# The routing ahead of an expert-choice layer: a table of bits on GpSimd, ties summed ahead of counts, the first expert's slot comparisons on two engines, and index products tile by tile

## The chip, the cores and the metric

The kernel runs on one core of a Trainium2 chip. The metric is device time in microseconds, as the median of several runs; lower is better. Matrix products run on TensorE (PE), elementwise work on VectorE (DVE), ScalarE (ACT) and GpSimd (POOL); SyncE (SP) issues most of the transfers.

## The reference, cut to what matters

The program is one layer of a diffusion backbone for 2048 latent and 128 context tokens of width 1024, all in fp32: modulation, a mixer of a long convolution and a retention branch, then an expert-choice mixture of 16 experts, then a final RMS norm. The change touches only the routing of the mixture:

```python
def ec_moe(h, p):
    T = B * L
    xt = h.reshape(T, D)
    aff = jax.nn.softmax((xt @ p["w_router"]).astype(F32), axis=-1)
    cap = (EC_CAPACITY_FACTOR * T) // N_EXPERTS          # 256 latent, 16 context tokens
    vals, idx = lax.top_k(aff.T, cap)                    # each expert picks its tokens
    xs = xt[idx]
    hid = silu(einsum("ecd,edf->ecf", xs, w_e_gate)) * einsum("ecd,edf->ecf", xs, w_e_up)
    ye = einsum("ecf,efd->ecd", hid, w_e_down) * vals[..., None]
    return zeros((T, D)).at[idx.reshape(-1)].add(ye.reshape(-1, D))
```

So for each expert the kernel must find the 256 latent and 16 context tokens of the largest probability, lowest token first among equals, and their numbers as a list that a gathering transfer can use.

## The kernel before

The program is a row of phases, each a block in which every engine has its own instruction stream; the streams meet only in semaphores. A helper class `Steps` counts one semaphore per list of named steps: `give` raises it once at the start by two rounds' worth, `inc` marks a step done, `at` is the value to wait for. All of the change lies in the last phase, `phase_experts`, and there ahead of the loop over experts.

The order there is fixed by hand, by the order of the instructions on each engine and the waits between them:

1. Entry. Each engine raises its own semaphores with `give`. DVE copies the probabilities into `arr` (three tiles of 128x128: latent, latent, context) and makes `spread` (step `as`); PE transposes the four tiles (L2697, L2698), so that a partition now holds an expert and an eighth of its tokens; DVE copies them to `prob`, sums `few`, and sets `thr`, `cand` and `bit`.
2. Threshold search, 15 rounds of two bits (`DIGITS`). The threshold is built as the bit pattern of a float. In a round DVE counts, for three candidate thresholds, how many latent probabilities reach each (L2940, three times, with the count accumulated into `cnt`), while POOL compares the context ones with theirs (L3162, three times 128x16, into `reach`). PE adds over partitions with a matrix `seg`: sixteen matmuls for the context (L2702) and one for the latent counts (L2705), in this order. DVE has meanwhile shifted `bit` right by two (L2943) and formed `rest`, the threshold so far with the bits of the three next candidates (L2946); when PE's sums are there it compares them with the capacities (L2949 for the context, L2952 for the latent ones), which gives the digit, then `step` (L2955), the next `cand` (L2957) and `thr` (L2959). POOL and DVE both wait for `cand`.
3. Above and ties. DVE counts what lies above the threshold (`gl`, `gc`, L2965), PE adds the counts (`above`, L2709), DVE subtracts them from the capacities (L2968), marks the ties (`tl`, `tc`, L2970) and makes running sums of them (L2976); the ends of these (L2980) go through PE (`ahead`), and L2985 takes that off `need` too (step `lim`). Then come the choice of ties, the running sums of all chosen tokens, their offsets, and a transpose on PE into `pos`: for each token and expert, how many chosen ones come up to it.
4. The first expert. For each of 16 tiles of 128 latent tokens DVE compares the 256 slot numbers with the position of the tile's tokens (`passed`, L3008, 128x256), then once 128x16 for the context (L3012). PE multiplies each result by ones, which counts for every slot the tokens below it and so gives the token's number (`index`, 32 matmuls L2722 and one L2724, all behind the last comparison). DVE copies the numbers to integers (`numbers`, L3023, L3024). POOL then does a one-element addition (`carry`, L3170), which serves as a step of its own stream, and starts three gathering transfers (L3183). The gathered tokens are transposed, split into high and low parts, and the products of expert 0 begin.
5. While the gather runs DVE makes the comparisons for the second expert. For later experts they are spread over the loop two experts ahead, three at a time.

Of the kernel before, what the change touches and what calls it, by code (L numbers as in the profile page):

```python
# [6 lines left out]
I32 = mybir.dt.int32  # L7
BF16 = mybir.dt.bfloat16
F32R = mybir.dt.float32r
ALU = mybir.AluOpType  # L10
# [4 lines left out]
P = 128  # L15
# [13 lines left out]
EPS = 1e-6  # L29
# [2489 lines left out]
def phase_experts(nc, d, s):  # L2519


    DIGITS = 15
    with ExitStack() as ctx:
# [10 lines left out]
        bit = sb("bit", [P, 2, 3], I32)  # L2534
# [59 lines left out]
        RB = counted("dve_bits", ["count", "bit", "next", "mc", "ml", "step", "cand", "thr"])  # L2594
        PB = counted("pool_bits", ["reach"])
        R1 = counted("dve_slots", ["gl", "gc", "need", "tl", "tc", "s0", "s1", "e0", "e1", "lim", "k0", "k1",
                                          "sel", "p0", "p1", "f0", "f1", "off", "q0", "q1", "pos", "ones"])
        QB, QC = counted("pe_bits", ["sum"]), counted("pe_bits_context", ["sum"])
        Q1 = counted("pe_route", ["prob", "above", "ahead", "slots", "pos"])
# [59 lines left out]
        with nc.Block() as block:  # L2659
# [29 lines left out]
            def _(pe):  # L2689
# [17 lines left out]
                for name, ready, half, src in (("above", "gc", 0, cnt[:, 0:2]), ("ahead", "e1", 1, ends[:]), ("slots", "f1", 1, ends[:])):  # L2707
                    pe.wait_ge(R1.sem, R1.at(0, ready))
                    pe.matmul(pi[:, 0:2], seg_b[:, P * half:P * half + P], src, start=True, stop=True)\  # L2709
                      .then_inc(*Q1.inc(name))  # L2710
# [6 lines left out]
                def index(e):  # L2717
                    pe.wait_ge(VM.sem, VM.at(e, "mc"))
                    pe.wait_ge(VI.sem, VI.at(e - 1, "i2"))
                    for half in range(2):  # L2720
                        for n in range(NLAT):
                            pe.matmul(pi[:, half:half + 1], below[:, n, P * half:P * half + P], ones[:],  # L2722
                                      start=(n == 0), stop=(n == NLAT - 1))
                    pe.matmul(pi[0:CCAP, 2:3], below_c[:], ones[:], start=True, stop=True).then_inc(*PI.inc("ids"))  # L2724
# [182 lines left out]
            def _(v):  # L2907
                for steps in (VG, VM, VI, VX, VK, VD, VW, VF, V0):
                    steps.give(v)
                v.sem_inc(VX.sem, KT)  # L2910
                v.memset(rms[:], 1.0).then_inc(*VF.inc("one"))
                v.memset(eps[:], EPS).then_inc(*VF.inc("eps"))
                for steps in (R0, RB, R1):
                    steps.give(v)
# [3 lines left out]
                for b in range(2):  # L2918
# [4 lines left out]
                                band[:].unsqueeze(1).broadcast_to([P, NE, 8]), ALU.mult).then_inc(*R0.inc("as"))  # L2923
                v.wait_ge(Q1.sem, Q1.at(0, "prob"))
# [4 lines left out]
                for j in range(3):  # L2929
                    v.memset(cand[:, :, j:j + 1], (j + 1) << (2 * DIGITS - 2))  # L2930
# [355 lines left out]
```

## Time and profile before

| what | value |
|---|---|
| median of 3 runs | 3420.57 us (3418.08 to 3425.08) |
| the profiled execution's own time | 3417.76 us |
| its span | 3415.5 us |
| PE busy | 3189.0 us (93%) |
| DVE busy | 1602.9 us (47%) |
| ACT busy | 1269.8 us (37%) |
| POOL busy | 375.8 us (11%) |

The span is the time from the first to the last instruction of one profiled execution; "busy" is the time in which an engine had an instruction in work. Instructions that only raise or await a semaphore are not busy time. The expert phase begins at about 2037 us of the span and the products of the first expert at about 2105 us; they take most of what follows. Times in the rows below are microseconds from the span's start; "mean" and the three numbers with slashes are nanoseconds.

### The profile page before, as it was taken

The numbers are of one execution on the slowest core, as the hardware profiler recorded it, in microseconds if no ns is written. First come the engines' busy times: TensorE is split into PE (matmuls) and PEld (weight loads), VectorE is DVE, ScalarE is ACT, GpSimd is POOL, SyncE is SP. The second block draws the span as 40 slices with busy tenths as digits, with TensorE's granted clock in tenths as the row PEclk, the third lists the DMA queues.
The fourth block names the chain that finished last, engine by engine and source line by source line (L and its number), as shares of the span: only waits on it lengthen the run. The fifth ranks groups of instructions, "written<-read, shape, count | busy, mean of one in ns | idle before, by whom it ended". The sixth has DMA issues, their size and how long they took to land. (4 is left out here: it accounts for less than half of the span.)

```text
span 3415.5 us, 51856 instructions
## 1 busy us (share of the span) xinstructions
PE 3189.0 (93%) x19543; PEld 2717.1 (80%) x19543; DVE 1602.9 (47%) x2955; ACT 1269.8 (37%) x1953; POOL 375.8 (11%) x358
## 2 busy tenths in 40 slices
PE   7899998999889699999989975999999999999996
PEld 2488887899745689989987764898888888899995
DVE  5423322433246442333225557555555555565556
ACT  4743442422243031222114542444444443444435
POOL 1011111000034100000000002111111111111122
PEclk9899999999999799999999986999999999999998
DMA  8633333322199761432115443555555555555557
GB/s 332 243 120 111 105 107 100 134 67 71 58 363 353 247 193 58 129 99 88 69 51 201 158 163 130 185 191 184 187 179 183 175 175 175 180 198 195 192 207 274
DMA packets 282678, 565.68 MB, mean 166 GB/s; under 512 B 23464, under 2 KB 162472, under 8 KB 278329
## 3 DMA queue, kind: packets, MB, share of 16 engines
q1 hardware_dynamic: 258063, 503.84, 42.7%
q0 software_dynamic: 15456, 54.88, 5.4%
q10 hardware_dynamic: 8976, 4.46, 0.4%
q8 instruction: 123, 2.02, 0.2%
q14 instruction: 60, 0.49, 0.0%
HBM read 434.45 MB, written 128.64 MB: 165 GB/s over the span
## 5 line engine op out<-in xcount | busy, mean ns | idle before, releaser
L71 PE MATMUL experts_bank<-experts_xT_high,experts_w_high_gu 128*128 128x272 f32 x2048 | 598.0, 292 | 6.2 <-DVE experts_w_low_gu L3032 5.5
L73 PE MATMUL experts_bank<-experts_xT_high,experts_w_low_gu 128*128 128x272 f32 x2048 | 591.9, 289 | 0.0
L72 PE MATMUL experts_bank<-experts_xT_low,experts_w_high_gu 128*128 128x272 f32 x2048 | 589.6, 288 | 0.0
L71 PEld LDWEIGHTS experts_bank<-experts_xT_high,experts_w_high_gu 128*128 128x128 f32 x2048 | 385.9, 188 | 19.5 <-issue 12.3
L72 PEld LDWEIGHTS experts_bank<-experts_xT_low,experts_w_high_gu 128*128 128x128 f32 x2048 | 387.1, 189 | 3.9
L73 PEld LDWEIGHTS experts_bank<-experts_xT_high,experts_w_low_gu 128*128 128x128 f32 x2048 | 386.0, 188 | 0.0
L3032 DVE TENSOR_TENSOR experts_w_low_gu<-experts_w_raw_gu,experts_w_high_gu 128x1024 fp32r<-128x1024 f32 x256 | 302.6, 1218 | 12.5 <-ACT experts_w_high_gu L2828 12.5
L2828 ACT ACTIVATE experts_w_high_gu<-experts_w_raw_gu 128x1024 fp32r<-128x1024 f32 x256 | 257.1, 1047 | 14.5 <-DMA experts_w_raw_gu<-in_w_stream 14.5
L71 PE MATMUL merge_pg<-merge_hT_high,merge_w_gates_high 128*128 128x436 f32 (+1 forms) x640 | 232.1, 363 | 12.0 <-DVE merge_hT_low L2097 12.0
L72 PE MATMUL merge_pg<-merge_hT_low,merge_w_gates_high 128*128 128x436 f32 (+1 forms) x640 | 231.3, 361 | 0.0
L73 PE MATMUL merge_pg<-merge_hT_high,merge_w_gates_low 128*128 128x436 f32 (+1 forms) x640 | 230.9, 361 | 0.0
L71 PE MATMUL experts_bank<-experts_w_high_d,experts_hid_high 128*128 128x512 f32 x512 | 209.7, 410 | 6.3 <-DVE experts_hid_low L3107 6.3
L72 PE MATMUL experts_bank<-experts_w_low_d,experts_hid_high 128*128 128x512 f32 x512 | 203.7, 398 | 0.0
L73 PE MATMUL experts_bank<-experts_w_high_d,experts_hid_low 128*128 128x512 f32 x512 | 202.2, 395 | 0.0
L71 PE MATMUL hyin_pz<-hyin_hT_high,hyin_w_high 128*128 128x436 f32 (+1 forms) x480 | 176.6, 368 | 16.1 <-DVE hyin_hT_low L1358 16.1
L3101 DVE TENSOR_TENSOR experts_full<-experts_bank,experts_act_g 128x256 f32<-128x256 f32 x128 | 54.4, 425 | 286.1 <-issue 143.9
L2071 ACT ACTIVATE merge_gate<-merge_pg 128x436 f32<-128x436 f32 (+1 forms) x80 | 41.4, 532 | 363.8 <-PE merge_pg L73 363.7
L73 PE MATMUL hyin_pz<-hyin_hT_high,hyin_w_low 128*128 128x436 f32 (+1 forms) x480 | 173.3, 361 | 0.0
L72 PE MATMUL hyin_pz<-hyin_hT_low,hyin_w_high 128*128 128x436 f32 (+1 forms) x480 | 173.1, 361 | 0.0
L3170 POOL TENSOR_TENSOR experts_spare<-experts_spare 128x1 f32<-128x1 f32 x46 | 51.3, 1127 | 1034.6 <-DVE experts_ye L3133 874.2
L2882 ACT ACTIVATE experts_hid_high<-experts_full 128x256 fp32r<-128x256 f32 x128 | 53.6, 419 | 283.5 <-DVE experts_full L3101 281.8
L2873 ACT ACTIVATE experts_act_g<-experts_bank 128x272 f32<-128x272 f32 x128 | 50.9, 398 | 289.1 <-PE experts_bank L73 286.8
(395 smaller groups left out, 6586.5 us busy)
## 6 DMA issues: line engine op xcount, KB each, us to landing
experts_w_raw_gu<-in_w_stream SPq DMA_DIRECT2D x256, 512.0 KB
experts_w_raw_d<-in_w_stream SPq DMA_DIRECT2D x128, 512.0 KB, 6.7
filters_wm<-in_w_mod SPq DMA_DIRECT2D x12, 2048.0 KB, 11.9
merge_hT<-scratch_hT SPq DMA_DIRECT2D x32, 436.0 KB, 7.3
scratch_h<-out_row SPq DMA_DIRECT2D x17, 520.0 KB, 3.0
x_early<-in_xs SPq DMA_DIRECT2D x17, 512.0 KB, 5.4
scratch_hT<-tokens_hT SPq DMA_DIRECT2D x17, 512.0 KB, 4.2
scratch_qkT<-tokens_qkT SPq DMA_DIRECT2D x17, 512.0 KB, 2.8
```

Source lines behind the costliest of these rows:

```text
L71: pe.matmul(out, lhs[0], rhs[0], start=start, stop=False)
L72: pe.matmul(out, lhs[0], rhs[1], start=False, stop=False)
L73: return pe.matmul(out, lhs[1], rhs[0], start=False, stop=stop)
L2071: act.activation(gate[:, c % 2, j, 0:n], pg[:, c % 2, j, 0:n], ACT.Sigmoid)\
L2828: act.activation(wh[kind][:, n % RINGS[kind], :], raw[kind][:, r, :], ACT.Copy).then_inc(*AW.inc(name))
L2873: act.activation(act_g[:], pg[:, 0:SLOTS], ACT.Silu).then_inc(*AG.inc(f"g{f}"))
L2882: act.activation(hh[:, f % 2, :], full[:, f % 2, :], ACT.Copy).then_inc(*AH.inc(f"h{f}"))
L3032: v.tensor_tensor(wl[kind][:, w, :], raw[kind][:, n % STAGES[kind], :], wh[kind][:, w, :].bitcast(F32), ALU.subtract).then_inc(*VW.inc(name))
L3101: v.tensor_tensor(full[:, f % 2, :], pu[:, 0:CAP], act_g[:, 0:CAP], ALU.mult).then_inc(*VG.inc(f"m{f}"))
L3170: g.tensor_tensor(spare[:, column:column + 1], spare[:, 0:1], spare[:, 0:1], ALU.add)\
```

## The change

There are five edits, all ahead of the loop over experts.

- The three bits of every round come from a table `unit` (14 rounds by 3 values) that POOL fills with 42 memsets at the start of the phase. The tile `bit`, its three memsets and its shift in every round are gone; DVE waits for the table once, ahead of the first round. The last round uses the last row again, as its `rest` is not read for another threshold.
- DVE raises only the semaphore `R0` before it begins; its other increments come behind the step `as`, two more behind `ones`, and the memsets of `rms` and `eps` behind the first expert's index copy. POOL's increments `CG` and `CP` come ahead of its rounds.
- The ties are marked and summed ahead of the counts. PE's sum of the ties goes to `pi`, that of the counts to another place in PSUM, `pn`.
- The first expert's comparisons are split: tiles 0 to 11 on DVE, 12 to 15 (`SPLIT` = 4) on POOL; the context's stays on DVE. PE waits for each tile by itself in its first sixteen matmuls.
- POOL's `carry` ahead of the first gather is replaced by an increment at the start.

```diff
+    SPLIT = 4
-        bit = sb("bit", [P, 2, 3], I32)
+        unit = sb("unit", [P, DIGITS - 1, 3], I32)
...
+        units, pool_below, dve_below = sem("units"), sem("pool_below_first"), sem("dve_below_first")
...
@@ PE
-                for name, ready, half, src in (("above", "gc", 0, cnt[:, 0:2]), ("ahead", "e1", 1, ends[:]), ("slots", "f1", 1, ends[:])):
+                for name, ready, half, src, to in (("ahead", "e1", 1, ends[:], pi), ("above", "gc", 0, cnt[:, 0:2], pn), ("slots", "f1", 1, ends[:], pi)):
                     pe.wait_ge(R1.sem, R1.at(0, ready))
-                    pe.matmul(pi[:, 0:2], seg_b[:, P * half:P * half + P], src, start=True, stop=True)\
+                    pe.matmul(to[:, 0:2], seg_b[:, P * half:P * half + P], src, start=True, stop=True)\
                       .then_inc(*Q1.inc(name))
...
                 def index(e):
-                    pe.wait_ge(VM.sem, VM.at(e, "mc"))
+                    if e:
+                        pe.wait_ge(VM.sem, VM.at(e, "mc"))
                     pe.wait_ge(VI.sem, VI.at(e - 1, "i2"))
                     for half in range(2):
                         for n in range(NLAT):
+                            if e == 0 and half == 0:
+                                if n < NLAT - SPLIT:
+                                    pe.wait_ge(dve_below, n + 1)
+                                else:
+                                    pe.wait_ge(pool_below, n - NLAT + SPLIT + 1)
                             pe.matmul(pi[:, half:half + 1], below[:, n, P * half:P * half + P], ones[:],
                                       start=(n == 0), stop=(n == NLAT - 1))
+                    if e == 0:
+                        pe.wait_ge(dve_below, NLAT - SPLIT + 1)
...
@@ DVE
-                for steps in (VG, VM, VI, VX, VK, VD, VW, VF, V0):
-                    steps.give(v)
-                v.sem_inc(VX.sem, KT)
-                v.memset(rms[:], 1.0).then_inc(*VF.inc("one"))
-                v.memset(eps[:], EPS).then_inc(*VF.inc("eps"))
-                for steps in (R0, RB, R1):
-                    steps.give(v)
+                R0.give(v)
                 v.memset(arr[:], 0.0).then_inc(*R0.inc("zero"))
...
+                for steps in (RB, R1, VG, VM, VI, VX, VK, VD, VW, VF, V0):
+                    steps.give(v)
                 v.wait_ge(Q1.sem, Q1.at(0, "prob"))
...
-                    mm = v.memset(bit[:, :, j:j + 1], (j + 1) << (2 * DIGITS - 2))
+                v.wait_ge(units, 1)
...
-                    v.tensor_single_scalar(bit[:], bit[:], 2, ALU.logical_shift_right).then_inc(*RB.inc("bit"))
                     v.wait_ge(RB.sem, RB.at(i - 1, "thr"))
-                    v.wait_ge(RB.sem, RB.at(i, "bit"))
-                    v.tensor_tensor(rest[:], thr[:].unsqueeze(2).broadcast_to([P, 2, 3]), bit[:], ALU.bitwise_or)\
+                    v.tensor_tensor(rest[:], thr[:].unsqueeze(2).broadcast_to([P, 2, 3]),
+                                    unit[:, min(i, DIGITS - 2), :].unsqueeze(1).broadcast_to([P, 2, 3]), ALU.bitwise_or)\
...
-                for n, name in enumerate(("gl", "gc")):
-                    v.tensor_scalar(parts(over, n), parts(prob, n), t(n), 0.0, ALU.is_gt, ALU.add,
-                                    accum_out=cnt[:, n:n + 1]).then_inc(*R1.inc(name))
-                v.wait_ge(Q1.sem, Q1.at(0, "above"))
-                v.tensor_tensor(need[:], caps[:], pi[:, 0:2], ALU.subtract).then_inc(*R1.inc("need"))
...
                 running(tie, "s", "e")
+                for n, name in enumerate(("gl", "gc")):
+                    v.tensor_scalar(parts(over, n), parts(prob, n), t(n), 0.0, ALU.is_gt, ALU.add,
+                                    accum_out=cnt[:, n:n + 1]).then_inc(*R1.inc(name))
                 v.wait_ge(Q1.sem, Q1.at(0, "ahead"))
-                v.tensor_tensor(need[:], need[:], pi[:, 0:2], ALU.subtract).then_inc(*R1.inc("lim"))
+                v.tensor_tensor(need[:], caps[:], pi[:, 0:2], ALU.subtract).then_inc(*R1.inc("need"))
+                done("need")
+                v.wait_ge(Q1.sem, Q1.at(0, "above"))
+                v.tensor_tensor(need[:], need[:], pn[:, 0:2], ALU.subtract).then_inc(*R1.inc("lim"))
...
                 done("ones")
+                v.sem_inc(VX.sem, KT)
+                v.sem_inc(VM.sem, NLAT + 1)
...
+                def passed_first():
+                    for n in range(NLAT - SPLIT):
+                        v.tensor_scalar(below[:, n, :], slot[:], pos[:, n % 2, n // 2:n // 2 + 1], None, ALU.is_ge)\
+                         .then_inc(dve_below, 1)
+                    v.tensor_scalar(below_c[:], slot[:, 0:CCAP], pos[:, 2, 0:1], None, ALU.is_ge).then_inc(dve_below, 1)
...
-                for n in range(NLAT):
-                    passed(0, n)
-                passed_context(0)
+                passed_first()
                 numbers(0, 0, 0)
+                v.memset(rms[:], 1.0).then_inc(*VF.inc("one"))
+                v.memset(eps[:], EPS).then_inc(*VF.inc("eps"))
...
@@ POOL
                 PB.give(g)
+                for i in range(DIGITS - 1):
+                    for j in range(3):
+                        mm = g.memset(unit[:, i, j:j + 1], (j + 1) << (2 * (DIGITS - 2 - i)))
+                mm.then_inc(units, 1)
+                CG.give(g)
+                CP.give(g)
+                g.sem_inc(*CG.inc("carry"))
...
-                    carry(CG, "carry", 1)
+                    if e:
+                        carry(CG, "carry", 1)
...
+                g.wait_ge(R1.sem, R1.at(0, "pos"))
+                for n in range(NLAT - SPLIT, NLAT):
+                    g.tensor_scalar(below[:, n, :], slot[:], pos[:, n % 2, n // 2:n // 2 + 1], None, ALU.is_ge)\
+                     .then_inc(pool_below, 1)
                 g.wait_ge(stored, 1)
                 gather(0, 0)
```

## Rows read from the trace of the kernel before

**Rows 1.** Busy time of the engines in three stretches; columns in the first line.

```profile
core 0: us, PE busy (x) PEld busy (x) DVE busy (x) ACT busy (x) POOL busy (x), PEclk, DMA share, GB/s
2038.40:2092.40 54.00, 12.88 (x298) 10.52 (x298) 45.99 (x285) 2.11 (x2) 13.54 (x45) 0.50 0.24 81
2092.40:2105.00 12.60, 6.00 (x58) 5.13 (x58) 9.70 (x25) 3.59 (x5) 3.19 (x4) 0.50 0.67 212
2105.00:2108.90 3.90, 3.90 (x18) 3.90 (x19) 3.02 (x9) 2.06 (x3) 2.74 (x3) 0.52 0.32 78
```

**Rows 2.** Timeline of DVE, entry: start, us, engine, line, operation [idle before].

```profile
2038.88 0.38 DVE L2915 MEMSET experts_ye<- 128x384 f32 x1 [0.33 <-issue]
...
2039.72 0.28 DVE L2922 TENSOR_TENSOR experts_ye<-aff,band 128x128 f32<-128x128 f32 x1
2041.22 0.56 DVE L2925 COPY experts_ye<-experts_bank 128x384 f32<-128x384 f32 x1 [1.21 <-PE experts_bank L2698]
...
2042.09 0.48 DVE L2940 TENSOR_SCALAR_CACHE_REDUCE experts_ye<-experts_ye,experts_cand 128x256 f32<-128x256 f32 x1
```

**Rows 3.** Line 44, `give`, at the entry: count, ns min/median/max, first and last start.

```profile
L44 DVEq EVENT_SEMAPHORE  x12: 21/21/21, 2037.5 to 2038.7; - x12
L44 PEldq EVENT_SEMAPHORE  x8: 51/51/51, 2037.5 to 2038.7; - x8
```

**Rows 4.** Timeline of POOL, its first instruction in the phase.

```profile
2037.45 0.10 POOL L3152 MEMSET experts_spare<- 128x4 f32 x1 [882.36 <-POOLq L2224]
```

**Rows 5.** Busy time by stretch: four memsets of POOL at the program's start.

```profile
0.26:0.45 0.19, 0.00 (x0) 0.00 (x0) 0.00 (x0) 0.00 (x0) 0.19 (x4) 1.00 0.00 0
```

**Rows 6.** Timeline of one round, DVE, POOL and PE (one of fifteen).

```profile
2044.25 0.17 DVE L2957 TENSOR_TENSOR experts_cand<-experts_step,experts_rest 128x6 int32<-128x6 int32 x1
2044.33 0.15 DVE L2959 TENSOR_TENSOR experts_thr<-experts_thr,experts_step 128x2 int32<-128x2 int32 x1
...
2044.51 0.90 POOL L3162 TENSOR_SCALAR experts_reach<-experts_few,experts_cand 128x16 bf16<-128x16 f32 x3 [1.43 <-DVE experts_thr L2959]
...
2045.47 0.59 PE L2702 MATMUL experts_bank<-experts_reach,seg 128*128 128x3 bf16 x16 [1.72 <-POOL experts_reach L3162]
...
2045.66 0.17 DVE L2943 TENSOR_SCALAR experts_bit<-experts_bit 128x6 int32<-128x6 int32 x1
2045.93 0.17 DVE L2946 TENSOR_TENSOR experts_rest<-experts_thr,experts_bit 128x6 int32<-128x6 int32 x1
2046.10 0.16 DVE L2949 TENSOR_SCALAR_CACHE_REDUCE experts_met<-experts_bank 128x3 f32<-128x3 f32 x1
```

**Rows 7.** Timeline of DVE: first count, tie tests, `lim`.

```profile
2077.70 0.48 DVE L2965 TENSOR_SCALAR_CACHE_REDUCE experts_ye<-experts_ye,experts_thr 128x256 f32<-128x256 f32 x1
...
2078.81 0.54 DVE L2970 TENSOR_SCALAR experts_ye<-experts_ye,experts_thr 128x256 f32<-128x256 f32 x2
...
2080.93 0.16 DVE L2985 TENSOR_TENSOR experts_need<-experts_need,experts_bank 128x2 f32<-128x2 f32 x1 [0.28 <-PE experts_bank L2709]
```

**Rows 8.** Timeline of DVE, PE and POOL: first expert's comparisons, index, first gather.

```profile
2086.39 4.29 DVE L3008 TENSOR_SCALAR experts_below<-experts_pos_slot 128x256 bf16<-128x256 f32 x16
...
2090.92 0.99 PE L2722 MATMUL experts_bank<-experts_ones,experts_below 128*128 128x1 bf16 x32 [5.19 <-issue]
...
2092.05 0.16 DVE L3023 CAST experts_ids<-experts_bank 128x2 int32<-128x2 f32 x1 [1.23 <-PE experts_bank L2724]
...
2092.40 0.19 POOL L3170 TENSOR_TENSOR experts_spare<-experts_spare 128x1 f32<-128x1 f32 x1 [16.15 <-issue]
2093.24 1.17 POOL L3183 DMA_INDIRECT experts_xg<-scratch_h,experts_ids  x1 [0.65 <-issue]
```

**Rows 9.** Timeline of POOL and DVE: one-element additions in the expert loop.

```profile
2189.68 3.03 POOL L3170 TENSOR_TENSOR experts_spare<-experts_spare 128x1 f32<-128x1 f32 x1 [79.21 <-DVE experts_ye L3133]
...
2191.79 0.86 DVE L3008 TENSOR_SCALAR experts_below<-experts_pos_slot 128x256 bf16<-128x256 f32 x3
...
3228.46 2.25 POOL L3170 TENSOR_TENSOR experts_spare<-experts_spare 128x1 f32<-128x1 f32 x1 [56.59 <-DVE experts_ye L3133]
```

**Rows 10.** Line 1075, a POOL operation of two SBUF inputs, an earlier phase.

```profile
L1075 POOL TENSOR_TENSOR tokens_vz<-tokens_vs,tokens_zeta x34: 1034/1040/1493, 167.9 to 582.1; 128x512 f32<-128x512 f32 x34
```

More of the change, by code:

```diff
@@ L2593, in phase_experts @@
         R0 = counted("dve_arrange", ["zero", "a0", "a1", "ac", "as", "prob", "few", "thr", "bit"])
-        RB = counted("dve_bits", ["count", "bit", "next", "mc", "ml", "step", "cand", "thr"])
+        RB = counted("dve_bits", ["count", "next", "mc", "ml", "step", "cand", "thr"])
         PB = counted("pool_bits", ["reach"])
-        R1 = counted("dve_slots", ["gl", "gc", "need", "tl", "tc", "s0", "s1", "e0", "e1", "lim", "k0", "k1",
+        units, pool_below, dve_below = sem("units"), sem("pool_below_first"), sem("dve_below_first")
+        R1 = counted("dve_slots", ["tl", "tc", "s0", "s1", "e0", "e1", "gl", "gc", "need", "lim", "k0", "k1",
                                           "sel", "p0", "p1", "f0", "f1", "off", "q0", "q1", "pos", "ones"])
         QB, QC = counted("pe_bits", ["sum"]), counted("pe_bits_context", ["sum"])
-        Q1 = counted("pe_route", ["prob", "above", "ahead", "slots", "pos"])
+        Q1 = counted("pe_route", ["prob", "ahead", "above", "slots", "pos"])
         PW = counted("pe_stream", STREAM + ["context"])
@@ L2929, in _ @@
                 for j in range(3):
-                    v.memset(cand[:, :, j:j + 1], (j + 1) << (2 * DIGITS - 2))
-                    mm = v.memset(bit[:, :, j:j + 1], (j + 1) << (2 * DIGITS - 2))
+                    mm = v.memset(cand[:, :, j:j + 1], (j + 1) << (2 * DIGITS - 2))
                 mm.then_inc(*R0.inc("bit"))
+                v.wait_ge(units, 1)
                 v.wait_ge(R0.sem, R0.at(0, "bit"))
@@ L3163, in _ @@
                     mm.then_inc(*PB.inc("reach"))
-                CG.give(g)
-                CP.give(g)
                 def carry(steps, name, column):
```

## The prediction

> **What bounds the kernel now.** I read the page's busy shares and chain first: TensorE (PE) is busy for most of the span and the expert products are the chain, so I asked where it is idle beside the changed code. The table of stretches answers: from 2038.4 to 2105.0, 66.6 us, PE works 18.9 us, at half clock, and VectorE (DVE) is busy for most of each stretch until 2092.4 [rows 1]. This is the routing. Nothing of the expert products can start before it has named the first expert's tokens, so a microsecond gained or lost there moves everything behind it by as much. All edits lie there; after 2105 PE has work without a gap and keeps what it is given.
>
> Then I read the stretch engine by engine, for which wait ends last at each step: the entry (an issue-bound DVE), fifteen rounds of the threshold search, one pass over ties and counts, the first expert's comparisons and the first gather.
>
> **Entry, 2037.5 to 2042.1.** DVE begins with twelve semaphore increments of 21 ns, spread from 2037.5 to 2038.7, two memsets between them [rows 3]. Its first useful work, the memset of `arr`, starts at 2038.88 [rows 2]. The change leaves one increment ahead of it. The last one at 2038.7 precedes the memset by some 0.15, so it can start near 2037.5 + 0.15 = 2037.65: 1.2 us earlier. PE's own eight increments also end at 2038.7 [rows 3]; `as` is then ready at 2039.72 + 0.28 - 1.2 = 2038.8, so both arrive together and 1.2 stands. The other eleven increments go behind `as`, at about 0.1 each 1.1 us, into DVE's wait of 1.21 for the transposes [rows 2]: hidden, and if the cover failed it would be tenths. Three memsets of `bit` go: their starts are hundredths apart, nothing. The rounds could start at 2042.09 - 1.2 = 2040.9.
>
> New is a wait for GpSimd's (POOL) table of 42 memsets. All of DVE's counting is queued behind it, and PE and the next rounds behind that. POOL's memset of `spare` starts at 2037.45 and lasts 0.10 [rows 4]; with an increment behind it the table can begin near 2037.9. No row shows memsets in such a number. The four at the program's start take 0.19 together [rows 5], so they start 0.03 apart. At 0.03 the table takes 1.3 us and is ready at 2039.2; at 0.10 it takes 4.2 and ends at 2042.1, which takes the 1.2 back; at the 0.30 of a POOL comparison (0.90 for three) it takes 12.6 and ends at 2050.5. I take 0.03, because it is the same operation on the same engine in a row. Three increments moved ahead of POOL's first comparison are 0.3 us in its slack of 1.6. Term: +1.2, from -8.5 to +1.2.
>
> **The fifteen rounds.** Each loses DVE's shift `bit` (0.17, and the wait for it: 2045.66 to 2045.93), 0.27 us, 4.0 in fifteen. But look at who sets the step after it. The comparison of the context sums (L2949) starts at 2046.10, 0.17 behind `rest`, while two small operations in a row start 0.08 apart (L2957 and L2959). It waits for PE: sixteen matmuls from 2045.47, 0.59 long, end at 2046.06, which leaves 0.04 for the semaphore. PE in turn waits for POOL's three comparisons of 0.90, which start at 2044.51, straight after the candidates (2044.25 + 0.17) [rows 6]. So candidates, POOL, PE, context comparison is a loop of 2.33 us that holds no `bit`; removing it lets `rest` end earlier and DVE wait longer. Term: 0. If PE's modelled end were not what it waits for, it is +4.0. Below nothing I see no price: the table's row is read where `bit` was.
>
> **Ties ahead of counts.** Before, the counts at 2077.70 are followed by PE's answer before the tie tests at 2078.81; the second answer releases L2985 at 2080.93 [rows 7]. After: tests at 2077.70; from them to the end of the first running sums' `ends` is what it was, so the counts start at 2077.70 + 1.8 = 2079.5 and last 0.8 to 2080.25; 0.05 to PE and 0.23 to DVE gives 2080.5. The tie sums' trip to PE (0.3) lies beside the counts. Term: +0.4, between 0 (the counts wait for something unseen) and +1.1 (the whole gap between counts and tests).
>
> **The first expert's comparisons.** Before: sixteen on DVE from 2086.39, 4.29 long, then context, then 32 matmuls from 2090.92 and the index copy at 2092.05: 5.66 us [rows 8]. After: two increments more ahead (0.2), twelve comparisons on DVE (0.26 apart, so 3.2), four on POOL, and PE follows tile by tile, so only some 21 matmuls of 0.029 stay behind. If the engines run side by side: 0.2 + 3.2 + 0.06 + 0.6 + 0.2 = 4.3, a gain of 1.4. That needs a POOL comparison of 128x256 below 0.88 us. None is in the trace: 128x16 takes 0.30, a multiplication of 128x512 1.04, so that 0.3 + 240 elements at (1.04 - 0.19)/511 us gives 0.7, my value [rows 6, 8, 10]; ends 0.30 and 1.04.
>
> But they hardly run side by side. At 2189.68 POOL's one-element addition, 0.19 long elsewhere, takes 3.03 us and ends at 2192.71; DVE then has subtractions of two SBUF operands and three comparisons of exactly this kind, until 2191.79 + 0.86 = 2192.65. Near the end, where no expert is left to compare for, at 3228.46, the same addition takes 2.25: shorter by 0.78, three comparisons at 0.26 [rows 9]. So a stream of these comparisons on DVE holds off a POOL operation that reads SBUF, to its last one. Against it stands one row: at 2092.40 such an addition took its 0.19 in the middle of DVE's comparisons [rows 8]. I take the hold. POOL, released by `pos` itself, comes first, DVE waits out its 0.7, then DVE's thirteen run through (3.4), and POOL's other three follow (0.4 without their start, and 0.7 twice): 5.9, then seventeen matmuls, the context's and the copy, 0.7: 6.6 instead of 5.66. Term: -0.9 (at 0.30 per comparison +0.7, at 1.04 -2.3); without the hold +1.4.
>
> SBUF — State Buffer of the Trainium skill, on the shared GpSimd/Vector port, has the rule: VectorE's two-port modes and GpSimd take that port pair exclusively, and whoever comes second is blocked for the whole instruction; `tensor_scalar` in fp32 is among the operations that enter such a mode. By that rule the gain of 1.4 is lost, as in my term. The trace agrees in the two additions of 3.03 and 2.25 us, and not in the one of 0.19. The GPSIMD Engine Reference (performance versus the Vector engine) gives about 1.03 cycles an element for such bodies at 1.2 GHz; by that estimate a POOL comparison is 0.5 us instead of 0.7, and the term about -0.1.
>
> **First gather.** The addition `carry` ahead of it goes: POOL at 2092.40, DMA at 2093.24 [rows 8]. It gives its own 0.19; at most the whole 0.84. Term: +0.2. The gather, transposes and splits behind it keep their distances. Two small memsets moved behind the index copy are 0.1 us into a stretch where DVE leads.
>
> **Sum.** 1.2 + 0 + 0.4 - 0.9 + 0.2 = 0.9 us. The profiled execution took 3417.76 us for a span of 3415.50, 2.8 below the median of 3420.57; a shift takes both alike: 3420.57 - 0.9 = 3419.7.
>
> **Rivals.** (a) No hold: DVE and POOL compare side by side. For it: the 0.19 at 2092.40. Then +1.4 in place of -0.9, 3.2 in all: 3417.4. (b) The rounds shorten by 0.27 each, since `bit` was on the path after all; for it that the busy row of `rest` touches the next without a gap, against it the 0.09 that this gap is too long: 4.9 with the hold, 3415.7, and 3413.4 with (a). (c) Slower: POOL's table is late. From 0.07 us a memset (2.9 us for 42) it eats the entry's gain, from 0.09 on the kernel is slower than before; at 0.10 3420.57 + 0.4 = 3421.0, at 0.30 3420.57 + 8.8 = 3429.4. For it: the 0.30 of POOL's other small operations; against it: the 0.19 for four [rows 5]. (d) The edits do what they say but PE's clock rises at another moment: PE is at half clock for the products' first 3.9 us as well (0.52), and later not [rows 1]; with it 1 or 2 us either way; it widens the range only.
>
> **Chances.** The forecast with the hold 0.52, (a) 0.34, (b) 0.08, (c) 0.06. A change below 0.2%, 6.8 us, can't be told from none here. The forecast, (a) and (b) with the hold lie within it; only (b) with (a), or an unseen gain on top, passes 3413.7: 0.07. Only (c) at its far end passes 3427.4: 0.03. Same: 0.90. The range: (a) at 3417.4 less a microsecond, and above, the hold at 1.04 per comparison (3421.1) with a late table or clock: 3416.0 to 3422.3.
>
> **What would show it.** The memset of `arr` near 2037.7 and the first count near 2040.9, not later (table); rounds still 2.33 apart, with DVE idle some 0.25 ahead of the context comparison; `lim` about 0.4 nearer to the last threshold; POOL's four comparisons: one near 0.7, the second over 3 us (hold) or four alike (a); the index copy 6.6 or 4.3 us after the first DVE comparison could start. The forecast is wrong if the products start more than 4 us earlier or any later than before, counted from the block's entry.

## The result and the profile after

| | before | after |
|---|---|---|
| median | 3420.91 us (3416.7 to 3425.08, 10 runs) | 3430.8 us (3427.5 to 3432.12, 10 runs) |
| ratio | | 1.0029 [1.0021, 1.0037] |
| profiled execution | 3417.76 | 3431.28 |
| its span, mean granted clock | 3415.5, 0.963 | 3429.5, 0.961 |

The changed kernel is slower by 9.9 us, and the interval of the ratio is clear of 1. The forecast was 3419.7, no difference that could be told.

First the stage that was edited. The timeline of the changed kernel: POOL's table, DVE's entry, one round, the ties and the first comparisons (columns as in [rows 2]).

```profile
2040.50 0.10 POOL L3167 MEMSET experts_spare<- 128x4 f32 x1 [883.98 <-POOLq L2224]
2040.76 1.54 POOL L3173 MEMSET experts_unit<- 128x1 int32 x42 [0.15 <-POOL experts_spare L3167]
...
2040.74 0.38 DVE L2919 MEMSET experts_ye<- 128x384 f32 x1 [2.12 <-PEq L2224]
2041.16 0.77 DVE L2923 COPY experts_ye<-aff 128x128 f32<-128x128 f32 x2
...
2044.50 0.48 DVE L2946 TENSOR_SCALAR_CACHE_REDUCE experts_ye<-experts_ye,experts_cand 128x256 f32<-128x256 f32 x1
...
2046.09 0.16 DVE L2954 TENSOR_SCALAR_CACHE_REDUCE experts_met<-experts_bank 128x3 f32<-128x3 f32 x1 [0.22 <-PE experts_bank L2704]
...
2079.49 0.55 DVE L2970 TENSOR_SCALAR experts_ye<-experts_ye,experts_thr 128x256 f32<-128x256 f32 x2
...
2082.34 0.16 DVE L2991 TENSOR_TENSOR experts_need<-experts_need,experts_bank 128x2 f32<-128x2 f32 x1 [0.28 <-PE experts_bank L2711]
...
2087.83 3.70 POOL L3209 TENSOR_SCALAR experts_below<-experts_pos_slot 128x256 bf16<-128x256 f32 x4 [9.78 <-DVE experts_ones L3008]
2088.01 4.71 DVE L3022 TENSOR_SCALAR experts_below<-experts_pos_slot 128x256 bf16<-128x256 f32 x12 [0.26 <-DVE experts_ones L3008]
```

Count from POOL's first memset in each kernel (2037.45 and 2040.50; no code ahead of it differs). The first count comes after 4.00 us instead of 4.64 [rows 2, 4], the first pass over the tokens after the rounds at 38.99 instead of 40.25 [rows 7], the index copy at 53.13 instead of 54.60 [rows 8]. So up to the copy the change gained 1.5 us. Then comes the copy (2093.63) and what follows it, on DVE, POOL and PE:

```profile
2093.63 0.16 DVE L3038 CAST experts_ids<-experts_bank 128x2 int32<-128x2 f32 x1 [0.77 <-PE experts_bank L2734]
...
2094.07 4.01 DVE L3016 TENSOR_SCALAR experts_below<-experts_pos_slot 128x256 bf16<-128x256 f32 x15
2098.01 0.22 DVE L3027 TENSOR_SCALAR experts_below_c<-experts_pos_slot 128x16 bf16<-128x16 f32 x1
2098.15 2.34 DVE L3047 TENSOR_TENSOR experts_w_low_gu<-experts_w_raw_gu,experts_w_high_gu 128x1024 fp32r<-128x1024 f32 x2
...
2094.78 3.45 POOL L3203 DMA_INDIRECT experts_xg<-scratch_h,experts_ids  x1 [3.25 <-issue]
2098.53 2.80 POOL L3203 DMA_INDIRECT experts_xg<-scratch_h,experts_ids  x1 [0.30 <-issue]
2101.63 0.85 POOL L3203 DMA_INDIRECT experts_xg<-scratch_h,experts_ids  x1 [0.30 <-issue]
...
2101.51 1.97 PE L2792 MATMUL experts_bank<-ident,experts_xg 128*128 128x128 f32 x8 [7.92 <-DMA experts_xg<-scratch_h,experts_ids]
2107.93 2.93 PE L2792 MATMUL experts_bank<-ident,experts_xg 128*128 128x128 f32 x16 [4.45 <-DMA experts_xg<-scratch_h,experts_ids]
...
2112.47 0.59 PE L71 MATMUL experts_bank<-experts_xT_high,experts_w_high_gu 128*128 128x272 f32 x1 [0.56 <-DVE experts_xT_low L3091]
```

POOL's first issue was 1.17 us long before [rows 8]; now it is 3.45 and the second 2.80. The first ends at 2098.23, when DVE's second-expert comparisons end (2098.01 + 0.22); the second ends 0.84 after DVE's subtractions (2098.15 + 2.34 = 2100.49). The two groups of transposes start 7.9 and 14.3 us after the copy; before, it was 5.6 and 8.35. So the first product comes 18.8 us after the copy instead of 12.9 (2104.94 in the trace of before), 5.9 us more, and the second group is what sets it. Its rows now arrive among the next weight loads: its transposes start 6.6 us after the end of its issue (2101.33), before it was 4.7 (2095.69 to 2100.40). The table of stretches of the changed kernel (columns as in [rows 1]):

```profile
2096.00:2099.00 3.00, 0.00 (x0) 0.00 (x0) 3.00 (x10) 0.00 (x0) 2.69 (x2) 0.50 0.05 7
...
2102.00:2106.00 4.00, 1.48 (x7) 1.08 (x6) 1.23 (x1) 1.02 (x1) 0.48 (x1) 0.50 1.00 390
```

Seven GB/s flow while the issue is held, and 390 when the rows at last compete. And then there is a loss in a place that nobody edited. DVE's context output, once per expert, marks the pace of the loop. Two in a row, from the timeline of the kernel before:

```profile
2188.32 1.27 DVE L3133 SCALAR_TENSOR_TENSOR experts_ye<-experts_ye,experts_vals,experts_gate 16x1024 f32<-16x1024 f32 x1 [4.47 <-ACT experts_ye L2893]
2268.23 1.27 DVE L3133 SCALAR_TENSOR_TENSOR experts_ye<-experts_ye,experts_vals,experts_gate 16x1024 f32<-16x1024 f32 x1 [4.47 <-ACT experts_ye L2893]
```

The same line of code in the changed kernel:

```profile
2196.87 1.27 DVE L3148 SCALAR_TENSOR_TENSOR experts_ye<-experts_ye,experts_vals,experts_gate 16x1024 f32<-16x1024 f32 x1 [4.47 <-ACT experts_ye L2903]
2277.13 1.27 DVE L3148 SCALAR_TENSOR_TENSOR experts_ye<-experts_ye,experts_vals,experts_gate 16x1024 f32<-16x1024 f32 x1 [4.47 <-ACT experts_ye L2903]
```

79.91 us an expert before, 80.26 now (means over thirteen periods: 79.907 and 80.260). The costliest groups of the page say on which engine (columns: busy us, mean ns, idle us before and its releaser). Before:

```profile
L71 PE MATMUL experts_bank<-experts_xT_high,experts_w_high_gu 128*128 128x272 f32 x2048 | 598.0, 292 | 6.2 <-DVE experts_w_low_gu L3032 5.5
```

The same group of the changed kernel:

```profile
L71 PE MATMUL experts_bank<-experts_xT_high,experts_w_high_gu 128*128 128x272 f32 x2048 | 602.6, 294 | 6.3 <-DVE experts_w_low_gu L3047 5.7
```

Idle time and count are the same, the products themselves are longer. It is not the clock: from 2400 to 3200 us PE is busy throughout and its granted clock is 1.00 in both traces. So the spans differ by 14.0 us thus: 3.05 from a later start of the block (it scatters from 2036.96 to 2043.68 over all profiled executions, and no code ahead of it differs, so it is counted as no part of the change), 4.5 from there to the first product (67.49 to 71.97), 1.0 in the first expert (83.38 to 84.40), 4.9 in the next fourteen, 0.5 at the end.

### The profile page after: what moved, and what is told of

The parts are those of the page before. It is cut to its first block and busy times, and to the rows that moved or that the text cites. A ratio compares the mean times of both kernels' runs of the same rounds, so it can differ in the third digit from the quotient of the medians.

```text
span 3429.5 us, 51867 instructions
## 1 busy us (share of the span) xinstructions
PE 3199.1 (93%) x19543; PEld 2725.8 (79%) x19543; DVE 1599.9 (47%) x2933; ACT 1270.1 (37%) x1953; POOL 386.2 (11%) x403
```

## The experiments

Two theories were set up from this. **Place**: the tile `unit` has 168 bytes a partition where `bit` had 24, and the rest of the phase's tiles lie behind it, 160 bytes further on (the products' moving tile `xT_high` from byte 157408 to 157568); PE's products with them are slower from there. **Held issue**: POOL's descriptor issue is held off by DVE's stream of comparisons. For each, a rival is in the expectations. In what follows "copy to product" is from the index copy to the first product, "issues" the first two durations of POOL's issue, "period" the mean distance of two experts.

**t1, the table put behind all other tiles**, with a hole of `bit`'s size left in its place.

```diff
-        unit = sb("unit", [P, DIGITS - 1, 3], I32)
+        hole = sb("hole", [P, 2, 3], I32)
...
         spare = sb("spare9", [P, 4])
+        unit = sb("unit", [P, DIGITS - 1, 3], I32)
```

> The changed kernel, with the table `unit` allocated behind all other tiles and a tile of the old size in its place, so that every other tile lies in SBUF where it lay before the change (xT_high at byte 157408 of a partition again, not 157568). Theory P (place): the 160 bytes by which the operands of the products moved slow PE by 0.5%. In the two traces an expert's period is 79.91 us before and 80.26 after, 0.35 us times 15 is 5.3 us of the 9.9. Then the period is 79.91 here, and the median about 3430.8 - 5.3 = 3425.5. Rival S (stream): the slower products come of the changed instruction stream of PE (17 more waits ahead of it, shifted fetches): then the period stays 80.26 and the median 3430.8.

Median 3426.38, ratio 1.0013 [1.0004, 1.0023]. Period 79.907, issues still 3.44 and 2.80. From its timeline:

```profile
2197.99 1.27 DVE L3149 SCALAR_TENSOR_TENSOR experts_ye<-experts_ye,experts_vals,experts_gate 16x1024 f32<-16x1024 f32 x1 [4.47 <-ACT experts_ye L2904]
2277.89 1.27 DVE L3149 SCALAR_TENSOR_TENSOR experts_ye<-experts_ye,experts_vals,experts_gate 16x1024 f32<-16x1024 f32 x1 [4.47 <-ACT experts_ye L2904]
```

**t2, the kernel before with `bit` as wide as the table.** No instruction differs from before.

```diff
-        bit = sb("bit", [P, 2, 3], I32)
+        bit = sb("bit", [P, 14, 3], I32)[:, 0:2, :]
```

> The kernel before, with the tile `bit` allocated at the size of the table (168 bytes a partition instead of 24) and used in its first two rows only; no instruction changes, but all tiles behind it move by 160 bytes as in the changed kernel. Theory P: period 80.26 us and about +5.3 us, 3426.2. Rival S: period 79.91 and 3420.9.

Median 3426.87, ratio 1.0018 [1.0009, 1.0028]; period 80.260, issues free (1.17, 0.97), first product 66.96 after the block's start. The place alone costs 6.0 by the medians and 15 x 0.353 = 5.3 by the periods. From its timeline:

```profile
2189.78 1.27 DVE L3133 SCALAR_TENSOR_TENSOR experts_ye<-experts_ye,experts_vals,experts_gate 16x1024 f32<-16x1024 f32 x1 [4.47 <-ACT experts_ye L2893]
2270.04 1.27 DVE L3133 SCALAR_TENSOR_TENSOR experts_ye<-experts_ye,experts_vals,experts_gate 16x1024 f32<-16x1024 f32 x1 [4.47 <-ACT experts_ye L2893]
```

**t3, `carry` back** (the changed kernel, with the one-element addition ahead of the first gather as before, and its increment at the start gone), and **t4, all sixteen comparisons on DVE** (`SPLIT` 4 to 0).

> The changed kernel with POOL's one-element addition put back ahead of the first gather. In the trace after the change the first two gathering transfers take POOL 3.45 and 2.80 us to issue, against 1.17 and 0.97 before, and from the index copy to the first product it is 18.8 us against 12.9. Theory C (carry): the addition ahead of it is what kept the issue short; then 1.2 and 1.0 again, 12.9 us, and about 3430.8 - 5.9 = 3424.9. Rival H (hold): the issue is held off by DVE's stream of the second expert's comparisons (it ends when that ends, at 2098.23, the second 0.84 after the subtractions' end), whatever POOL did before: then 3.4 and 2.8 stay, 3430.8 or a little more. Rival O (POOL's own comparisons just ahead): stays as well.

> The changed kernel with SPLIT = 0: DVE makes all sixteen comparisons of the first expert, POOL none; PE still goes tile by tile. Rival O: POOL's comparisons just ahead of the gather are what makes its issue long (they are another operation of POOL, and the issue is its first since): then 1.2 and 1.0 us, about 3430.8 - 5.9 = 3424.9. Theory C and rival H: the issue stays at 3.4 and 2.8. In all of them the comparisons take 4.2 us instead of 4.7 and the index copy comes about 5.1 us after they start (5.6 in the trace after).

t3: 3426.45, ratio 1.0012 [1.0002, 1.0021]; t4: 3427.05, 1.0014 [1.0005, 1.0024]. In both the issues are free (1.17, 0.97 and 1.16, 0.96), copy to product is 12.86 and 12.54, and the period stays 80.26. Either edit takes the second fault away, by 4.3 and 3.8 us of median. What the two have in common is that they shift moments and change what POOL does last before the issue, so more runs were needed.

**u1, u2, u3: what holds the issue.** One execution each, of variants of the changed kernel. u1 lets DVE wait for the gathered rows ahead of its second-expert comparisons; u2 has POOL raise a semaphore once ahead of the gather, without touching SBUF; u3 a memset there.

```diff
+                for each in g0:
+                    v.wait_ge(each, 16)
                 for n in range(NLAT):
                     passed(1, n)
@@ u2
+                    else:
+                        g.sem_inc(pc, 1)
@@ u3
+                    else:
+                        g.memset(spare10[:, 1:2], 0.0)
```

> The changed kernel, but DVE waits for all three gathering transfers before it starts the second expert's comparisons; POOL's first gather has the SBUF port it shares with DVE to itself. Theory H (hold): DVE's stream is what makes the first two issues 3.45 and 2.80 us long; without it they take about 1.0 to 1.2 each, the first transposes start some 5.6 us and the second near 7.9 us behind the index copy, although no addition stands ahead of them. The comparisons and subtractions (6.6 us) then fall behind the gather, so the products still start late, about 17 us behind the copy. Rival A (the addition does something for the issue itself, a first call for instance): the issues stay at 3.4 and 2.8.

> The changed kernel with one semaphore increment of POOL where the addition stood, some 0.05 to 0.1 us of delay and no access to SBUF. The issue started 1.15 and 1.16 us behind the index copy in the two kernels where it was held (the changed one, and the one with the table last), and 1.19 to 1.25 in the four where it was not; DVE's comparisons come every 0.26. Theory M (moment): it depends on where in DVE's beat the issue asks for the port; then the shift changes the outcome, to 1.2 and 1.0 us, and products 12.9 us behind the copy. Rival W (what POOL did last): with POOL's comparisons as the last work on SBUF the issue is held whatever the moment: 3.4 and 2.8.

> The changed kernel with a one-element memset of POOL (which writes SBUF and reads none of it) where the addition stood. Rival W: any access of POOL to SBUF in between clears it, so 1.2 and 1.0 us; if only a read does, 3.4 and 2.8. Theory M: the memset takes 0.10 us, a shift of 0.05 to 0.1, and the outcome depends on that alone, as in the kernel with the increment: the two come out alike.

u1, 3428.79: issues 1.17 and 0.96, started 1.15 after the copy as in the changed kernel. Without DVE's stream beside it the issue, started at a moment that was held there, is not held. (The stream then delays DVE's part of the first tokens, so copy to product is still 17.57.) u2, 3424.02: free, started at 1.19; u3, 3430.06: held (3.41, 2.79), started at 1.18. The timeline of u2 on POOL:

```profile
2094.67 1.17 POOL L3205 DMA_INDIRECT experts_xg<-scratch_h,experts_ids  x1 [3.29 <-issue]
2096.14 0.96 POOL L3205 DMA_INDIRECT experts_xg<-scratch_h,experts_ids  x1 [0.30 <-issue]
```

With an increment that moved the issue by 0.04 us it was free. That is one execution; x1 below shows that the same start can fall either way, so the 0.04 is not shown to be the cause.

**u4, both faults taken away**: t1 and t4 together.

> Both causes taken out of the changed kernel: the table allocated last (place as before) and SPLIT = 0 (DVE makes all comparisons of the first expert). From the traces so far: products 65.2 us behind POOL's first memset of the phase against 67.5 before, period 79.91 as before, so 3420.9 - 2.3 = 3418.6, from 3417 to 3420. If the two causes are not all there is, it stays above 3420.9.

Median 3419.73 (11 runs), ratio 0.9997 [0.9988, 1.0006]: as fast as before, 11 us under the changed kernel. Issues 1.16 and 0.96, period 79.907, first product 65.32 after the block's start, 2.2 us earlier than before. The first expert then takes 84.34 to its context output instead of 83.38, which gives 1.0 of the 2.2 back.

**v1, s1, s2: the moment again**, u4 with four, one and two of u2's increments ahead of the first gather. POOL has no comparisons in any.

> The kernel with the table last and no comparison on POOL, with four semaphore increments of POOL ahead of the first gather. Its issue would start near 1.25 + 4 x 0.04 = 1.41 us behind the index copy (one increment moved it by 0.04). So far the issue was held in the four kernels where it started at 1.15 to 1.18 and free in the seven at 1.16 without a stream, 1.19 and 1.25; DVE's comparisons repeat every 0.26, so the held moments would come again at 1.41 to 1.44. Theory M (moment alone): held here, issues of 3.4 and 2.8 us, though POOL made no comparison at all and nothing else is changed. Rival W (POOL's comparisons as its last access are needed as well): free, 1.2 and 1.0.

> The kernel with the table last and no comparison on POOL, with one increment of POOL ahead of the first gather. Free at none (1.25 us behind the index copy), held at four (1.51). Theory M (moment): the outcome follows the start of the issue, with some border between; at one increment, near 1.3, I expect it free if the border lies above, held if below; products 12.7 or 19.4 us behind the copy, nothing in between. A rival that would break M: intermediate issues, 2 us for instance.

> The same with two increments, start near 1.38. By M again one of the two outcomes; with the one-increment kernel it says on which side the border lies. If held moments repeat with DVE's 0.26 (held at 1.15 to 1.18, so again at 1.41 to 1.44, and 1.51 is 1.25 one beat later, which was free), then free here and at one; the four-increment kernel already speaks against that simple rule.

3421.8, 3423.82 and 3426.76, one execution each. All three held: first issues 3.09, 3.32 and 3.24, started 1.51, 1.28 and 1.36 after the copy, where u4's at 1.25 was free; copy to product 19.4 to 20.1. So POOL's comparisons are no condition of the hold, and to be late does not help either. A rule by DVE's beat of 0.26, on which v1 was expected to be held, fell: by it s1 and s2 should have been free. The timeline of s1 on POOL:

```profile
2092.40 3.32 POOL L3207 DMA_INDIRECT experts_xg<-scratch_h,experts_ids  x1 [16.35 <-issue]
2096.03 2.80 POOL L3207 DMA_INDIRECT experts_xg<-scratch_h,experts_ids  x1 [0.30 <-issue]
```

**w1, w2, w3, x1, x2: which place.** The kernel before with a tile `pad` of so many bytes a partition ahead of `xT_high` (w1 32, w3 64, x2 96, x1 160), or of 160 bytes behind `xT_low` (w2). In the diff, x2:

```diff
+        pad = sb("pad", [P, 24])
         xh = sb("xT_high", [P, 2, KT, SLOTS], F32R)
```

> The kernel before with an unused tile of 32 bytes a partition ahead of xT_high: xT_high starts at byte 157440, a multiple of 64 as in the changed kernel (157568), where before it is 32 past one (157408); xT_low likewise. Theory X: it is the operands xT_high and xT_low of the gate and up products, and whether they start at a multiple of 64 bytes or 32 past one: period 80.26 us. Rival Y: the distance of 160 bytes or another tile's place decides: period 79.91, or a third value.

> The kernel before with an unused tile of 160 bytes behind xT_low: all tiles behind it (act_g, full, hid_high, ye and on) move as in the changed kernel, and xT_high and xT_low stay. Theory X: period 79.91. If the tiles behind (the operand hid_high of the down products, the outputs of DVE and ACT) carry the loss: 80.26.

> The kernel before with 64 unused bytes ahead of xT_high: 157472, again 32 past a multiple of 64. Theory X: period 79.91. If it is the multiple of 128 that counts (157440 and 157568 both are; 157472 is not), this run can't tell it from X, but a third period would show that the place matters more finely.

> The kernel before with 160 unused bytes ahead of xT_high, which brings xT_high, xT_low and all behind them to where the changed kernel has them (157568); the tiles ahead of xT_high stay. The period was 79.91 us at +0, 79.93 at +32, 80.03 at +64 and 80.26 with everything behind `bit` at +160; with only the tiles behind xT_low at +160 it was 79.93. Theory X2 (place of xT_high and xT_low): 80.26. If the tiles between `bit` and xT_high (below, ids, xg) carry it: near 79.93.

> As above with 96 bytes (157504). If the loss grows with the distance from the old place (0.03 at 32, 0.12 at 64, 0.35 at 160), the period is between 80.03 and 80.26, near 80.1; if it depends on a smaller unit that repeats, it may be back at 79.9.

| bytes ahead of `xT_high` | 0 | 32 | 64 | 96 | 160 | 160 behind `xT_low` |
|---|---|---|---|---|---|---|
| period, us | 79.907 | 79.933 | 80.027 | 79.740 | 80.320 | 79.927 |
| of it 128x272 products | 48.59 | 48.86 | 48.68 | 48.87 | 48.91 | 48.56 |
| of it 128x512 products | 22.98 | 22.74 | 22.98 | 22.52 | 23.04 | 23.02 |
| one execution, us | (before) | 3421.03 | 3423.12 | 3418.61 | 3434.83 | 3420.23 |

The two middle rows split the period by kind of product (each PE instruction counted from its start to the next one's, mean of twelve periods). The 128x272 products are the gate and up products, with `xT_high` and `xT_low` as moving tiles; the 128x512 ones are the down products, with `hid_high` and `hid_low` as weights, which lie behind `xT_low`. What is left, 8.3 us, is the same to 0.04 in all.

Moving only what lies behind `xT_low` by 160 bytes costs 0.02 us a period, moving the tokens' tiles with it 0.41. So x1's loss is that of the place of `xT_high` and `xT_low`. The rule expected for the bad places, a start at a multiple of 64 bytes, seemed to fall with w1, whose period hardly moved, and x2 came out below both values expected for it. But the period is a sum of two effects. By the 128x272 products alone the rule sorts all the places tried: 48.86 to 48.91 at the three multiples of 64 (32, 96 and 160 bytes on from 157408, which is 32 past one), 48.56 to 48.68 at the others; the changed kernel has 48.90. What hides it are the down products, 0.24 faster in w1 and 0.46 in x2. The pages show both, before and then x2:

```profile
L72 PE MATMUL experts_bank<-experts_w_low_d,experts_hid_high 128*128 128x512 f32 x512 | 203.7, 398 | 0.0
...
L71 PE MATMUL experts_bank<-experts_xT_high,experts_w_high_gu 128*128 128x272 f32 x2048 | 603.3, 295 | 6.9 <-DVE experts_w_low_gu L3033 5.9
L72 PE MATMUL experts_bank<-experts_w_low_d,experts_hid_high 128*128 128x512 f32 x512 | 201.0, 393 | 0.0
```

x2's products with `xT_high` are as slow as the changed kernel's (294 there, 292 before); it gains in the down products alone. Which tile's place sets those is not shown: w2 moved `hid_high` too and left them at 23.02, and no run moved it alone by 96.

x1 brought something else: its instructions are those of before, and yet its first issue was held, through the comparisons and the subtractions (which ended at 2100.72). The same stream of instructions, started 1.19 after the copy, was free in before, t2, w1, w2, w3, x2 and y2: it can fall either way. The timeline of x1 on POOL:

```profile
2094.25 0.19 POOL L3171 TENSOR_TENSOR experts_spare<-experts_spare 128x1 f32<-128x1 f32 x1 [16.15 <-issue]
2095.09 6.68 POOL L3184 DMA_INDIRECT experts_xg<-scratch_h,experts_ids  x1 [0.65 <-issue]
```

**y1, y2: the good place, timed.** u4 with the 96 bytes of x2, and x2 once more.

> The table last and SPLIT 0, as in the best version so far, with 96 bytes a partition ahead of the tile xT_high. Theory of the place: experts 79.74 us apart, as in the kernel before with the same 96 bytes, instead of 79.907; fifteen periods make 2.5 us, and the entry, rounds and ties keep their 1.6: 3420.6 - 2.5 - 1 = 3417.1 if the first gather's issue is free (1.17 and 0.97 us), 3422 if it is held (over 3 us). Rival, the place's price is a property of one build or one run and not of the place: 79.9 apart and about 3419.7.

> The kernel before with nothing but 96 bytes a partition ahead of the tile xT_high. Theory of the place: experts 79.74 us apart and 3420.6 - 2.5 = 3418.1, told from the kernel before by the intervals of this many rounds. Rival: the one look before fell on a good run, and the median is that of the kernel before, 3420.6.

y1: 3417.61 (3413.14 to 3422.09, 11 runs), ratio 0.9991 [0.9982, 1.0001]. y2: 3418.41 (3413.81 to 3420.38, 11 runs), 0.9991 [0.9982, 1.0000]. Their periods are 79.740 both, as x2's, so the place's effect repeats to the thousandth. Both medians lie 2 to 3 us under before (3420.45 beside them), about what 15 x 0.167 = 2.5 gives, but with intervals that reach 1, so neither is told from before by its time; y1 is the lowest of all, and not told from y2.

## Why the prediction was wrong

Its sum was a gain of 0.9; the median came 11.1 above the forecast, and above 3427.4, to which it had given a chance of 0.03. Step by step, before to after, by the traces:

- **Entry, predicted +1.2: +0.64.** The table cost what was said (42 memsets in 1.54, 0.037 apart) and was never late. But DVE's two copies, 0.44 long in the kernel before, took 0.77 while it ran, and the copy and multiplication behind them 0.49 and 0.42 instead of 0.18 and 0.28. So it is in all twelve kernels with the table and in none without. The cost of filling beside DVE was left out. (That it is the filling is argued from the overlap: no run had the other edits without the table.)
- **Rounds, 0: +0.62.** The loop did keep its 2.33 (fifteen are 35.0), and DVE idles 0.22 to 0.28 ahead of the context comparison, as predicted. The gain is two longer rounds of before, by 0.29 and 0.24, which all eight kernels with its instructions have and no other has, and 0.08 in the first round. The term was right as to the loop and lucky in sign.
- **Ties, +0.4: +0.38.** Right.
- **First expert's comparisons, -0.9: -0.17**, and both cases missed how. POOL's four took 0.92 each and DVE's twelve 4.71 instead of 3.2, with two of DVE's to one of POOL's while POOL's ran (0.45 each) and 0.26 each after them: neither a hold to the end of the stream nor side by side, but turns. PE followed tile by tile, which gave back what was lost.
- **First gather, +0.2: -5.95.** "The gather, transposes and splits behind it keep their distances" is the first step that failed. Taking out `carry` brought the issue only 0.04 nearer to the copy (1.19 to 1.15), and there it was held. The row on which it rested, 1.17 beside a DVE stream [rows 8], was one outcome of two. I had used that stream's hold against a POOL addition [rows 9] in the term above and did not ask the same of the issue one line further down.
- **After the first product, "keeps what it is given": 6.4 more**, 5.3 of them fifteen periods at 0.353. The second step that failed, and the list of parts with it: "all edits lie there" counted instructions, not declarations. `unit` in the place of `bit` moved every tile behind it (t1 and t2: the period goes with the place and not with the instructions).
- Rival (c), a late table, was on the right side for a cause that did not occur. Rival (d) was there in small: the first four microseconds of products have a granted clock of 0.52 before and 0.50 after, the next four 1.00 and 0.82. That is about 0.8 us at full speed, and with the longer products it makes the 1.0 of the first expert. It comes with the edits: in eleven of the twelve kernels that have them the second four are at 0.75 to 0.92 and the first expert takes 83.76 to 84.40 (u1 has 1.00 and 83.38), in the eight with before's instructions 0.93 to 1.00 and 82.99 to 83.57. The sum had no term for it.

The two faults by themselves are 5.3 and 5.9 us by the traces; taken out one at a time they gave 4.4 (t1) and 4.3 and 3.8 (t3, t4) of median, give or take some 3 us each, and together, with the split undone as well, 11.1 (u4). What then remains is 2.2 us up to the first product less 1.0 in the first expert, too small to be told: u4 is 0.9 under the 3420.6 of before beside it, well inside its interval. That its 3419.73 is the forecast's 3419.7 is chance: it has no split, and its terms are others.

SBUF — State Buffer of the Trainium skill ("A bandwidth-pool intuition that's wrong (but worth ruling out)") says that a transfer whose descriptors GpSimd writes waits until a VectorE operation frees the shared port, and then ends some 0.12 us behind it. The trace agrees in kind (2.80, 3.45 and 6.68 us for 0.97 and 1.17). But with a stream of short operations it does not decide here: of nineteen profiled kernels with the stream beside the issue twelve had it free, before's among them, and seven held, and the ends lay 0.00, 0.84 and 1.05 behind DVE's.

Left open: what decides whether the issue is held. By its start, 1.15, 1.16, 1.18, 1.28, 1.36 and 1.51 were held, 1.25 was not in three kernels, 1.19 was in one kernel of ten. Each is one profiled execution; only where ten runs or more were made (the changed kernel and t1 held; before, t2, t3, t4, u4, y1 and y2 free) do the medians fit with its being so in most. Open too is why PE's products depend on the place of a tile. If the two effects of the table are independent, moving only what lies behind `xT_low` by 96 bytes would give an estimated 79.907 - 0.46 = 79.45 a period; no run tried it.

## What to carry to other kernels

A tile that grows moves all that are declared behind it: put new tiles last, as t1 did, and if a loop that nobody touched runs at another pace, compare addresses before instructions. Ahead of a GpSimd-issued transfer that a chain waits for, keep VectorE free of long streams of SBUF comparisons, or count the transfer at its held price; one profile that shows it short proves nothing. Putting the stream behind the transfer only helps if nothing waits for what follows the stream: u1 freed the issue and still had its first product 17.57 after the copy. And where a total does not follow a rule, split it by kind before you drop the rule. A count of instructions is not the list of what a change changes.

## What the hardware showed that I had not expected

- 128x272 fp32 products took 0.6% longer (48.86 to 48.91 us an expert for 48.59) with their moving tiles at the three places tried that are multiples of 64 bytes, and the 128x512 products behind them up to 2% less (22.52 for 22.98), repeatably; the periods of 79.74 to 80.32 are the sums.
- VectorE's fp32 copies took longer beside GpSimd's memsets, which read nothing (0.77 for 0.44).
- GpSimd and VectorE comparisons of one kind took turns (0.92 and 0.45 each), where a like stream held an issue or an addition to its end.
